# Two groups of table loads issued earlier, and norm columns taken from modulation rows, in a one-core fp32 kernel of four layers

## The reference

```python
# first block, layer 0 (even) and layer 1 (odd)
sh1, sc1, gt1, sh2, sc2, gt2 = ada_params(c, w_ada[layer], b_ada[layer])   # silu(c) @ w + b, six rows of 1024
# layer 0
h = modulate(rmsnorm(x, g_mix), sh1, sc1)           # h * (1 + scale) + shift
x = x + gt1 * (concat([hyena(h), neighborhood_attention(h)]) @ w_mix_out)
x = x + gt2 * swiglu(modulate(rmsnorm(x, g_ffn), sh2, sc2), ffn_w1, ffn_w3, ffn_w2)
# layer 1
x = x + gt1 * (fourier_mix(modulate(rmsnorm(x, g_mix), sh1, sc1)) @ w_fourier)
x = x + gt2 * moe_swiglu(modulate(rmsnorm(x, g_ffn), sh2, sc2), w_router, b_router, moe_w1, moe_w3, moe_w2)
x = rmsnorm(x, final_g)
# second block: the same scheme, norm without a gain
x = x + g1 * retention_mixer(rms_norm(x) * (1 + sc1) + sh1)
x = x + g2 * conv_ffn(rms_norm(x) * (1 + sc2) + sh2)
x = x + g1 * s5_mixer(rms_norm(x) * (1 + sc1) + sh1)
x = x + g2 * conv_ffn(rms_norm(x) * (1 + sc2) + sh2)
return rms_norm(x) * final_norm_g
```

## Time and profile before

| | us |
|---|---|
| median of 3 runs | 2465.39 (2463.64 to 2472.26) |
| the profiled execution | 2464.37 |
| its span, first to last instruction | 2462.5 |
| PE busy | 2293.7 (93%) |
| PE weight loads busy | 1584.6 (64%) |
| DVE busy | 1135.5 (46%) |
| ACT busy | 741.9 (30%) |
| POOL busy | 217.7 (9%) |
| mean granted TensorE clock | 0.973 |

### The profile page before, as it was taken

How to read it: one execution, slowest core, us unless ns; L and a number is a source line. 1 busy time by engine, 2 the same in 40 slices (tenths; PEclk the granted TensorE clock), 3 DMA queues, 4 the chain that set the end, 5 groups by cost and what they waited for, 6 DMA issues and landing times.

```text
span 2462.5 us, 40397 instructions
## 1 busy us (share of the span) xinstructions
PE 2293.7 (93%) x16841; PEld 1584.6 (64%) x16841; DVE 1135.5 (46%) x1851; ACT 741.9 (30%) x1125; POOL 217.7 (9%) x247
## 2 busy tenths in 40 slices
PE   6998999999888899999999999989989998898998
PEld 2774659984333243237776777678668986555996
DVE  3404645542520111004544555375456768994673
ACT  2100534432100000004433444344345542103552
POOL 0400410001000000000000000000000044650000
PEclk9999999999989999999999999989999999999999
DMA  7825447557699999999999899945648555604552
GB/s 291 195 93 234 100 138 247 187 189 317 247 387 410 413 405 409 413 416 344 393 393 394 300 393 393 363 132 190 239 145 280 183 189 165 276 1 162 181 186 79
DMA packets 254499, 644.76 MB, mean 262 GB/s; under 512 B 12559, under 2 KB 102832, under 8 KB 234296
## 3 DMA queue, kind: packets, MB, share of 16 engines
q1 hardware_dynamic: 248152, 627.86, 69.0%
q0 software_dynamic: 5584, 12.28, 2.5%
q10 hardware_dynamic: 592, 2.15, 0.2%
HBM read 641.18 MB, written 1.05 MB: 261 GB/s over the span
## 4 chain that ended last, share of the span: by engine, by line
PE 74%; DMA 15%; DVE 6%; issue 2%; ACT 1%; POOL 1%; SPq 0%; DVEq 0%; POOLq 0%; ACTq 0%
DMA ring<-in_moe_w 13%; PE bank L1868 7%; PE bank L1885 5%; PE bank L1886 5%; PE bank L1887 5%; PE bank L1896 4%; PE bank L1895 4%; PE bank L1897 4%; PE bank L965 3%; PE bank L811 3%; PE bank L967 2%; PE bank L966 2%; PE bank L1929 2%; PE bank L2322 2%; PE bank L857 2%; PE bank L745 2%
## 5 line engine op out<-in xcount | busy, mean ns | idle before, releaser
L1406 DVE TENSOR_TENSOR w_low<-ring,w_high 128x1024 fp32r<-128x1024 f32 x168 | 198.6, 1221 | 179.4 <-ACT w_high L1145 179.4
L2800 DVE TENSOR_TENSOR ring_low<-ring,up_high 128x1024 fp32r<-128x1024 f32 x186 | 226.6, 1276 | 112.9 <-ACT up_high L2439 112.7
L1885 PE MATMUL bank<-ht_low,up_high 128*128 128x256 f32 x960 | 271.0, 282 | 0.0
L1145 ACT ACTIVATE w_high<-ring 128x1024 fp32r<-128x1024 f32 x168 | 169.9, 1054 | 238.9 <-DMA ring<-in_moe_w 185.0
L2439 ACT ACTIVATE up_high<-ring 128x1024 fp32r<-128x1024 f32 x186 | 182.6, 1046 | 83.5 <-PE bank L1897 72.7
L1885 PEld LDWEIGHTS bank<-ht_low,up_high 128*128 128x128 f32 x960 | 180.3, 188 | 1.6 <-DVE arena L2676 0.8
L1886 PE MATMUL bank<-ht_high_cf_up,up_high 128*128 128x256 f32 x640 | 180.1, 281 | 0.0
L1887 PE MATMUL bank<-ht_high_cf_up,ring_low 128*128 128x256 f32 x640 | 178.1, 278 | 0.0
L1868 PE MATMUL bank<-HT,ring 128*128 128x256 f32 x704 | 159.1, 389 | 6.4 <-ACT HT L2414 4.7
L1868 PEld LDWEIGHTS bank<-HT,ring 128*128 128x128 f32 x704 | 137.0, 196 | 28.9 <-ACT HT L2414 9.3
L745 PE MATMUL bank<-ring,arena 128*64 128x512 f32 (+1 forms) x512 | 105.5, 547 | 22.9 <-DMA ring<-in_moe_w 22.9
(11 more groups left out here) (477 smaller groups left out, 4131.5 us busy)
## 6 DMA issues: line engine op xcount, KB each, us to landing
ring<-in_moe_w SPq DMA_DIRECT2D x336, 1024.0 KB, 13.2
ring<-in_w_ada SPq DMA_DIRECT2D x48, 1024.0 KB, 7.2
ring<-in_ada_w SPq DMA_DIRECT2D x48, 1024.0 KB, 5.1
ring<-in_ffn_w_up SPq DMA_DIRECT2D x44, 1024.0 KB, 5.1
ring<-in_ffn_w SPq DMA_DIRECT2D x33, 1024.0 KB, 5.3
ring<-in_ret_w_in SPq DMA_DIRECT2D x24, 1024.0 KB, 5.3
ring<-in_ffn_w_down SPq DMA_DIRECT2D x22, 1024.0 KB, 4.9
ring<-in_w_in SPq DMA_DIRECT2D x12, 1024.0 KB, 9.5
```

The source lines that it names most:

```text
L1406: dve.tensor_tensor(out=WL[half % SPLIT][:, :], in0=slot(i)[:, HALF * (q % 2):HALF * (q % 2) + HALF], in1=WH[half % SPLIT][:, :], op=ALU.s ...
L1885: pe.matmul(o, high, HT_LOW[:, k, :], start=k == 0, stop=False)
L2800: dve.tensor_tensor(out=low_of(base + tile, q), in0=slot(base + tile)[:, HALF * q:HALF * q + HALF], in1=high_of(part, n), op=ALU.subtract) ...
```

## The change

It has four parts.

1. **Fourier tables.** `FOD` and `FOL` are issued by POOL when PE has used the last weight tile of ffn's up half, no longer when `X` has been updated at the end of ffn.
2. **Router tables.** The four router tables are issued at the end of ffn (`x_ready` 2), no longer at the end of the Fourier stage (`x_ready` 3); they get another place in SBUF (columns 20672 on of `arena`), which is free by then.
3. **Norm columns.** For the norms four, ret and s5 a new `first_columns` makes shift and scale columns straight from the modulation rows: four products whose weights are 128-column pieces of `MODR` (or `G`) and whose moving operand is four columns of the identity. The spreads of (1, 0), (2, 0) and (3, 0) and their evacuations go, with the waits for them. The norms ffn, cf0 and cf1 keep the old way.
4. **End of the experts.** The last `add_scattered` signals after each half of the tokens, and ACT starts on the first half at the first signal. DVE takes the columns of ret ahead of the scaling by `final_g`, no longer behind it. PE no longer waits for `moe_added`.

```diff
-        SPREADS = [(0, 0), "ctx", (0, 1), (0, 2), (1, 0), (1, 1), (1, 2), (2, 0), (2, 1), (2, 2), (3, 0), (3, 1), (3, 2)]
-        BY_ACT = ((2, 0), (3, 1), (3, 2))
+        SPREADS = [(0, 0), "ctx", (0, 1), (0, 2), (1, 1), (1, 2), (2, 1), (2, 2), (3, 1), (3, 2)]
+        BY_ACT = ((3, 1), (3, 2))
...
-        WR = at(15680, KD, EXPERTS)
-        BR8 = at(15744, EXPERTS)
-        IOTA, IOTAN, IOTAX, BEFORE = (at(15752 + P * i, P) for i in range(4))
+        WR = at(20672, KD, EXPERTS)
+        BR8 = at(20736, EXPERTS)
+        IOTA, BEFORE, IOTAN, IOTAX = (at(20744 + P * i, P) for i in range(4))
...
             gain("moe", A["norm_g"][1, 1])
-            pool.wait_ge(sem("x_ready"), 3)
-            pool.dma_start(WR, A["w_router"]).then_inc(sem("route_landed"), 16)
-            pool.dma_start(BR8, bcast(A["b_router"][0])).then_inc(sem("route_landed"), 16)
-            pool.dma_start(IOTA, A["t_iota"]).then_inc(sem("route_landed"), 16)
-            pool.dma_start(BEFORE, A["t_before"]).then_inc(sem("route_landed"), 16)
             gain("fin0", A["final_g"])
...
             pe.matmul(PS[2][:, 0:1], ident[:, :], ones[:, 0:1], start=True, stop=True).then_inc(sem("moe_done"), 1)
-            pe.wait_ge(sem("moe_added"), 1)
...
             dve.wait_ge(sem("moe_done"), 1)
-            add_scattered().then_inc(sem("moe_added"), 1)
-            dve.wait_ge(sem("moe_added"), 1)
+            for t in range(TT):
+                add_scattered(t).then_inc(sem("moe_added"), 1)
+            dve.wait_ge(sem("moe_added"), TT)
...
             gain("four", A["norm_g"][1, 0])
-            pool.wait_ge(sem("x_ready"), 2)
+            sa.wait_done(pool, sa.first["ffn_down"] - 1)
             pool.dma_start(FOD, A["t_four_d"]).then_inc(sem("four_landed"), 16)
             pool.dma_start(FOL, A["t_four_l"]).then_inc(sem("four_landed"), 16)
+            pool.wait_ge(sem("x_ready"), 2)
+            pool.dma_start(WR, A["w_router"]).then_inc(sem("route_landed"), 16)
+            pool.dma_start(BR8, bcast(A["b_router"][0])).then_inc(sem("route_landed"), 16)
+            pool.dma_start(IOTA, A["t_iota"]).then_inc(sem("route_landed"), 16)
+            pool.dma_start(BEFORE, A["t_before"]).then_inc(sem("route_landed"), 16)
             pool.wait_ge(sem("mod_spread"), spread_at((1, 2)))
...
+            def first_columns(a, given=None):
+
+                pe.wait_ge(sem("modr_ready"), 3 * a + 1)
+                r = 2 * (a > 1)
+                for c in range(4):
+                    mm = pe.matmul(PS[3][:, 4 * c:4 * c + 4], mod_row(a, 0)[:, P * c:P * c + P], ident[:, r:r + 97:32], start=True, stop=True)
+                if given is not None:
+                    for k in range(KD):
+                        mm = pe.transpose(PS[3][:, 16 + k:17 + k], given[0:1, P * k:P * k + P], ident[0:1, 0:1])
                 mm.then_inc(sem("cols_turned"), 1)
...
-            gated_ffn(sa, "ffn_up", "ffn_down", HID_FFN, lambda: mod_spread(1, 0, 0, 4))
+            gated_ffn(sa, "ffn_up", "ffn_down", HID_FFN)
 
             rows_behind(sa, 1, 1, 1, 0, 3)
-            mod_taken((1, 0))
             pe.wait_ge(sem("gain_landed"), 16 * (GB_LOADS["four"] + 1))
-            turn_columns(PS[3], ada_part(1), ada_part(0), G)
+            first_columns(1, G)
...
-            mod_spread(2, 0, 1)
-            mod_taken((2, 0))
-            turn_columns(PS[3], ada_part(1), ada_part(0))
+            first_columns(2)
             turn("ret")
...
-            gated_ffn(sbm, "cf_up0", "cf_down0", HID_CF[0], lambda: mod_spread(3, 0, 1, 4))
-
-            mod_taken((3, 0))
-            turn_columns(PS[3], ada_part(1), ada_part(0))
+            gated_ffn(sbm, "cf_up0", "cf_down0", HID_CF[0])
+
+            first_columns(3)
             turn("s5")
...
+                    elif part == "moe_added":
+                        act.wait_ge(sem(part), t + 1)
...
-                    if j == 2 and spread:
-                        mod_evac(spread, ada_part(0), 4)
...
             moe_scalar(act, ch)
-            act.wait_ge(sem("moe_added"), 1)
-            norm_stats(X)
-            mod_evac((2, 0), AD[:, 0:2 * D])
-
+            norm_stats(X, 1, part="moe_added")
             norm_stats(X, 4)
...
-                link(dve.tensor_copy(SHIFT_COLS, o[:, 8:16]))
-                if how == "load":
+                if how == "first" or how == "first load":
+                    parts_of = o[:, 0:16].rearrange("p (c i k) -> p i k c", c=4, i=2)
+                    shift, scale = parts_of[:, 0], parts_of[:, 1]
+                    to_shift, to_gain, given = (v.rearrange("p (k c) -> p k c", k=2) for v in (SHIFT_COLS, GAIN_COLS, GIVEN_COLS))
+                else:
+                    scale, shift, to_shift, to_gain, given = o[:, 0:8], o[:, 8:16], SHIFT_COLS, GAIN_COLS, GIVEN_COLS
+                link(dve.tensor_copy(to_shift, shift))
...
-                    if j == 2 and spread:
-                        mod_evac(spread, ada_part(1), 4)
...
+            take_columns("ret", "first")
             dve.wait_ge(sem("gain_landed"), 16 * (GB_LOADS["fin0"] + 1))
             for t in range(TT):
                 inverse_rms("fin0", t)
                 stt(X[:, t, :], X[:, t, :], rinv[:, t:t + 1], G[:, :], ALU.mult, ALU.mult, sem("x_ready") if t else sem("x_first"))
 
-            mod_here((2, 0))
-            take_columns("ret", "scale")
             normalise("ret")
```

28 lines of the change are left out of this document (13 added, 15 removed).

## The result

The changed kernel took 2446.17 us (median of 5 runs, 2441.97 to 2449.61) beside 2463.64 for the kernel before in the same rounds (2462.25 to 2472.26): a ratio of 0.992, 95% interval 0.9906 to 0.9933. That is 17.5 us by the medians, 19.7 by the ratio and 16.5 to 23.2 by its interval; 15.9 were forecast (2449.5, range 2444 to 2457). Its profiled execution took 2446.17 too, with a span of 2444.3, 18.2 less than before. Over all executions of this study, 62 of the kernel before average 2464.8 and 17 of the changed one 2445.3, each single one off its average by 3.6 us (one standard deviation): 19.5 us less, with a standard error of 1.0. So the direction and most of the sum were right, and the forecast was some 3.5 us too small.

What follows compares the result with a forecast made beforehand. Nearly every stage was taken as PE-bound, the experts as DMA-bound. Terms 3.65 + 1.9 + 2.55 + 1.8 + 2.1 + 0.1 + 3.8 = 15.9 us, off 2465.39, gave 2449.5 us, range 2444 to 2457.

Steps and rivals of the forecast that it cites:

- the term of 2.1 us for the two spreads: In ffn and cf0, one removed spread each no longer holds up PE: 2.1 us together, bounds 0 and 2.3.
- The four terms for the tables: Fourier products: 3.65 us of wait, 1.9 of slow clock; router products: 2.55 of wait, 1.8 of slow clock.
- the one for the end of the experts: From the experts' last additions to retention's first turn: 3.8 us sooner, bounds 3.0 and 5.5.
- both clock terms: Fourier and router products run at full clock once their waits go: 1.9 us (bounds 0 to 1.9) and 1.8 (0 to 1.8).
- cf0's case: At cf0's start, after 0.58 us of waiting, 64 records took 14.05 us, full clock; assumed for the Fourier and router products.
- The rival of the low clock: Clock stays low behind both the Fourier and router waits: price 3.7 us, giving 2453.2; chance 0.14.
- that of late tables: Fourier tables don't land sooner because DVE's work holds up POOL's loads; first two terms lost, 2455.1; chance 0.03.
- The one of modulation tiles: Near the router, the last modulation-row tiles land too late: gives back up to 4.35 us, 2453.9; chance 0.12.
- The lower bound's reason: Experts to retention: saving only 3.0 us if retention tables, issued 1.3 us earlier but wanted 3.8 earlier, come late.
- The upper bound's reason: Experts to retention: saving 5.5 us if PE keeps its clock.
- I leave that: Retention's first weight tiles took 15.63 us against 14.05 at low clock; the forecast counted no change there.
- The rival of more: More than forecast: 2447 us if PE's clock holds between the experts and retention; chance 0.09.

Runs made afterwards that it cites:

- the two single-part kernels: Kernel before with only the Fourier tables issued earlier: 2459.41 us, ratio 0.9987; kernel before with only the router tables issued earlier and moved: ratio 0.9972.
- the first control: The changed kernel run again with nothing changed: median 2444.6 us, ratio 0.9918 to the kernel before.
- the second: The changed kernel run again unchanged a second time, on another chip: median 2444.6 us, ratio 0.9919 to the kernel before.

## Where the prediction was right, and which step of it failed

The mechanisms of the large terms were right. The step that failed is the term of 2.1 us for the two spreads, 1.07 each: the runs showed 1.35 to 2.2 in ffn and 2.4 in cf0, 3.7 to 4.6 in all. The four terms for the tables were met to 0.5 in all, the one for the end of the experts to 0.03.

*Tables.* The four terms for waits and clock were 9.9 us, and 9.42 were measured at their places; the two single-part kernels repeated 5.42 and 3.60. The choice of the upper bound for both clock terms, by cf0's case, was right: with 0.58 and 0.90 us of waiting left, the clock stayed at 1.00. The rival of the low clock is out, and that of late tables too. The one of modulation tiles came true in a mild form: PE now waits 1.5 us in all for `in_ada_w` behind the router, but ahead of a wait of 3.9 us for DVE that is there in both kernels, so it costs nothing: from the end of the router products to the gathering of the narrow experts' tokens 20.05 us pass, 20.04 before. The Trainium skill ("SBUF — State Buffer", the section on the two separate sides) gave the rival of the late Fourier tables its mechanism. The two issues took 0.54 and 0.53 us, as ever, and no delay of a stage came of it; but DVE ran only an addition with one operand in PSUM beside them, so the rule wasn't put to the test there.

*Spreads.* Part of the shortfall is the price of one spread on PE, read from its start to the next record's start. Before, the record ahead of it starts at 390.90, the one behind it at 392.18 and the next at 392.40; neighbours start 0.12 apart elsewhere, so the spread holds PE up for 1.26 us. The run with the spreads put back agrees (190.80 against 189.53). The rest is no price of a spread: up to 0.85 in ffn, of open cause, and 1.1 in cf0 from how DVE's splits meet POOL's instructions, of which the prediction said nothing; it stood in no row that it had read.

*Experts to retention.* 3.8 forecast, 3.83 measured, with 1.20 for the halves. The lower bound's reason, late retention tables, was right as a mechanism and wrong as a size, 0.3 in place of 0.8, and it acted on the wait behind the first tiles, not on the turn. The upper bound's reason, PE's clock, came true only in part: the first tiles took 14.05 in seven of the ten profiles of the changed kernel and its variants and 15.4 to 16.1 in three. "I leave that" was the right choice by its outcome: the stretch from the turn to cf0 was 242.1 to 242.7 us in the four profiles with the late turn and 242.2 to 242.7 in the three of the changed kernel. The prediction gave no reason for it, so this is luck. The rival of more (2447) rested on this clock; the measured 2446.17 is near its price, and its reason isn't what made it. By its own bound of 5.5 the price would have been 2447.8.

*Experts.* 0 forecast, 3.81 seen in the first pair of profiles, at most about 0.7 on average. Reading that pair alone would have given the change a gain that it doesn't have. That the pair's spans differ by 18.2 is in part luck: some 3.1 too much from the experts, 2.0 too little from the start of ffn.

*The sum.* What the places show to be the change's own is 9.4 + 1.35 to 2.2 + 2.4 + 3.8, so 17.0 to 17.8 us, and up to 0.7 from the experts. The executions say 19.5 with a standard error of 1.0. The upper end is within twice that error, so a further gain of 1 to 2 us is neither found nor shown; with single places that swing by up to 3 us between executions, fifteen profiles can't settle it.

## What to carry to other kernels

A wait ahead of dense products can cost twice: its length, and then the half clock at which the first products run; the second part was half to two thirds of the first here (1.70 beside 3.54, 1.68 beside 2.50), and both are read from the trace. Where a wait can't go, dummy products can keep the clock, if they leave only a short gap and are done before the wait ends; started when the clock has already fallen, they only delayed. And a faster start counts only as far as the stage behind it is bound by PE: retention gave its 1.6 us back. Last, before a gain of a few us is given to an edit, look at how the same stretch differs between two profiles of the same program.

## What the chip showed beyond that

- **POOL and DVE hold each other up.** DVE's scaling of 128 x 1024 from SBUF to SBUF takes 0.75 us alone, 1.84 and 2.06 beside POOL's fills; its subtraction of the same size 1.22 alone, up to 2.94 beside POOL's products; the update of `X` (two operands from SBUF) 0.69 alone and 2.25 beside POOL's products. POOL's issue of a load takes 0.54 alone, 0.87 and 1.00 beside the scaling, 0.53 beside the additions from PSUM. The Trainium skill ("SBUF — State Buffer", the section on the two separate sides) says that the two share a pair of ports, which one of them takes for a whole instruction; these numbers agree with it, on both sides: each engine was slowed beside the other.
- **Gaps and PE's clock.** Full clock (2.4 GHz) survived gaps of 0.58, 0.90, 1.43 and, behind the turns, 1.76 us; half (1.2 GHz) followed gaps of 2.11, 2.49, 3.40 and 4.61 us. All lie in light work, so these are cases and no rule. The length of the gap alone doesn't decide: in the middle of S5 the clock stayed full behind a gap of 1.51 us in the first control and fell behind one of 1.50 in the second, the same program.
